# One decoder layer on one core: x loaded once, squares summed on TensorE, gates in four column groups, memory keys 512 wide, heads five chunks apart

## The chip, the cores and the metric

The kernel runs on 1 core of one Trainium2 chip. The metric is the device time of one execution in microseconds (us); the kernel before takes 1358.43 us, the median of 3 runs (1358.29 to 1359.12). A difference of 0.2% (2.7 us) is about the least that a measurement of this kernel can tell from none.

## What is computed

One inference step of a hybrid decoder layer, for 256 prompt tokens and 8 x 4 decode tokens together (288 columns), model width 2048:

```python
h = rms_norm(x, norm_mix); proj = h @ w_in          # qk_m, v_m, o_m, 4+4 gates, q_a, k_a, v_a
qk_m = silu(conv(qk_m)); h_m, C, n, m = mlstm_chunkwise(q_m, k_m, v_m, ig, fg, C0, n0, m0)   # 4 heads
h_m = rms_norm(h_m) * sigmoid(o_m)
a_out = window attention of q_a, k_a (both QK-normed), v_a, with sinks and relative bias
x = x + concat(h_m, a_out) @ w_out
x = x + cross_attend(rms_norm(x), mem_k, mem_v)     # mem_k = rms_norm(rms_norm(mem) @ wk), mem_v likewise
x = x + square(relu(rms_norm(x) @ w_up)) @ w_down   # d_ff 8192
```

Besides y it returns the new states (conv rows, C, n, m, window keys and values, memory keys and values).

## The kernel before

Activations lie transposed in SBUF (features on partitions, 16 feature tiles "kt" by 288 tokens). All weights come as a **stream** of 388 chunks of 512 KB (four 128 x 256 tiles each), in the order in which they are used. A float32 product is made of three fp32r products: each chunk is split into whi (ACT, line 1010) and wlo (DVE, line 1467, the residue), each activation tile into hi (ACT, line 992) and lo (DVE, line 1453). One chunk is then 4 kt x 3 products x 2 output tiles = 24 matmuls of 288 columns (PE, `chunk`, line 520). Four chunks make one pair of output tiles, held in PSUM banks `g`; DVE copies them out (with the factor rstd). The chunk ring has 4 places.

The order is written by hand. Each engine runs a loop over chunks c. In turn c, which I call **slot c**, PE multiplies chunk c and then does what the table `beside[c]` lists; ACT and DVE first split chunk c+3 (ACT waits until PE has released chunk c-1, and for the DMA) and then do their part of `beside[c]`; at the end of every fourth slot DVE copies out the finished tiles. Each engine takes its own instructions strictly in order, so whatever stands late in one slot holds up the split of the next.

Chunks 0 to 7 are the memory keys (`wk_x`; tokens on the output's partitions, so matmuls are 256 wide here), chunks 8 to 11 the attention keys and values (the first use of x), 12 to 27 the queries, 28 to 59 conv, q/k and values of the mLSTM heads, 60 to 75 the output gate, 76 to 107 `w_out`. Beside the first of them stand these steps:

- `mem_prep`, `x_prep(kt)`: hi and lo of a tile of the memory tokens and of x. PE waits tile by tile for them in the first chunks of each (`each`). x_prep stands two to a slot in slots 2 to 9.
- `x_squares`, slots 10 to 12: the token sums of x squared, by ACT from a second copy of x with tokens on partitions (`xtok`, `xdec`); DVE puts them on a diagonal, and `norm_x` (slot 12) spreads them over the partitions by one matmul; ACT takes the root (line 997), DVE the reciprocal (line 1456) into `rstd`.
- `gates_mm` (slot 12): 32 matmuls with hi and lo of x; then `gates_a` (DVE, ends with `nz`, line 1453), `gates_ln` (ACT: Exp, then Ln), `gates_b`, `gates_c` (DVE), `gates_exp` (ACT, ends `gate_rows`).
- `k_norm` (slot 15): ACT squares the keys, PE sums them by a matmul with `blk`, ACT root, DVE reciprocal; then `keys_turn` (17), `keys_rev` (19; both transpose keys, DVE copies them between), `columns` (20).

The mLSTM heads h stand at slots 60+4h: `m_exps`, `m_scores(h)` with `m_turn` and `m_gate` of head h-1, then `m_num(h)` one slot later, `m_state`, `m_root`, and `m_expo(h+1)` in the fourth. m_num(h) uses a PSUM bank that m_gate(h-1) reads. On DVE the split of slots 64, 68 and 72 stands after m_scores' operations and not first (`heads`). After the last output tile x is loaded again for the residual by POOL (`xT_in`); DVE waits for it when the first pair of w_out's tiles is ready.

The SP queue issues the stream, mixed with memory tokens (2 MB), x (2.25 MB), gate weights, constants, the second copy of x (2.25 MB) and the memory's second copy; a chunk's load waits for the split that frees its place.

## Time and profile before

| | us |
|---|---|
| median of 3 runs | 1358.43 |
| the profiled execution's own time | 1360.29 |
| its span on the core | 1358.5 |
| PE, DVE, ACT, POOL busy | 1330.5, 819.9, 622.7, 97.7 |
| 388 splits on DVE, on ACT, busy | 476.1, 408.5 |
| granted clock of TensorE, mean | 0.999 |

The span is one execution on the core; 1.8 us of the profiled time lie outside it. Busy times overlap between engines. Matmul ends are modelled: starts are what to read, and two matmuls of 288 columns start 0.27 us apart in a full stream. A row in brackets names what ended the idle time before an instruction.

### The profile page before, as it was taken

The numbers are of one execution on the slowest core, as the hardware profiler recorded it, in microseconds if no ns is written. First come the engines' busy times: TensorE is split into PE (matmuls) and PEld (weight loads), VectorE is DVE, ScalarE is ACT, GpSimd is POOL, SyncE is SP. The second block draws the span as 40 slices with busy tenths as digits, with TensorE's granted clock in tenths as the row PEclk, the third lists the DMA queues.
The fourth block names the chain that finished last, engine by engine and source line by source line (L and its number), as shares of the span: only waits on it lengthen the run. The fifth ranks groups of instructions, "written<-read, shape, count | busy, mean of one in ns | idle before, by whom it ended". The sixth has DMA issues, their size and how long they took to land.

```text
span 1358.5 us, 27261 instructions
## 1 busy us (share of the span) xinstructions
PE 1330.5 (98%) x10213; PEld 1301.3 (96%) x10213; DVE 819.9 (60%) x1240; ACT 622.7 (46%) x889; POOL 97.7 (7%) x139
## 2 busy tenths in 40 slices
PE   7999999999999997999999999999999999999999
PEld 7998989978999987999999999999999999999999
DVE  7767888888666466665444565444555444565443
ACT  7674666667444455543333343333343333343331
POOL 0031001111423202000000000000000000000000
PEclk9999999999999999999999999999999999999999
DMA  9687445665944963655545555555555545555543
GB/s 381 254 227 249 132 140 184 192 216 171 374 157 154 292 224 105 216 157 168 170 162 162 168 157 170 171 161 163 168 157 169 170 158 166 165 160 171 170 158 128
DMA packets 75276, 251.87 MB, mean 185 GB/s; under 512 B 8332, under 2 KB 17376, under 8 KB 74560
## 3 DMA queue, kind: packets, MB, share of 16 engines
q1 hardware_dynamic: 59184, 215.49, 48.3%
q0 software_dynamic: 15744, 35.07, 8.2%
q8 instruction: 40, 0.66, 0.2%
q10 hardware_dynamic: 288, 0.48, 0.1%
q14 instruction: 20, 0.16, 0.0%
HBM read 238.00 MB, written 13.63 MB: 185 GB/s over the span
## 4 chain that ended last, share of the span: by engine, by line
PE 80%; DVE 10%; ACT 4%; issue 3%; DMA 3%; SPq 0%; DVEq 0%; ACTq 0%
PE g L520 77%; PE m L520 3%; DVE arena L1453 3%; DMA raw<-in_stream 2%; DVE wlo L1467 2%; ACT arena L992 2%; DVE arena L1450 2%; ACT whi L1010 1%; DVE b_lo L1453 0%; DVE arena L1446 0%; DVE arena L1442 0%; DMA arena<-in_memT 0%; ACT a_hi L992 0%; DVE arena L1456 0%; ACT b_hi L992 0%
## 5 line engine op out<-in xcount | busy, mean ns | idle before, releaser
L1467 DVE TENSOR_TENSOR wlo<-raw,whi 128x1024 fp32r<-128x1024 f32 x388 | 476.1, 1237 | 375.4 <-ACT whi L1010 363.4
L1010 ACT ACTIVATE whi<-raw 128x1024 fp32r<-128x1024 f32 x388 | 408.5, 1060 | 475.3 <-PE g L520 438.6
L520 PE MATMUL g<-a_hi,whi 128*128 128x288 f32 x1632 | 355.7, 299 | 1.5 <-ACT a_hi L992 1.5
L520 PE MATMUL g<-a_lo,whi 128*128 128x288 f32 x1632 | 349.7, 295 | 0.0
L520 PE MATMUL g<-a_hi,wlo 128*128 128x288 f32 x1632 | 348.4, 295 | 0.0
L520 PE MATMUL g<-b_hi,whi 128*128 128x288 f32 x1344 | 289.3, 297 | 5.6 <-DVE arena L1450 5.4
L520 PE MATMUL g<-b_lo,whi 128*128 128x288 f32 x1344 | 288.0, 295 | 0.0
L520 PE MATMUL g<-b_hi,wlo 128*128 128x288 f32 x1344 | 286.5, 294 | 0.0
L520 PEld LDWEIGHTS g<-a_hi,whi 128*128 128x128 f32 x1632 | 261.0, 188 | 8.4 <-issue 5.4
L520 PEld LDWEIGHTS g<-a_lo,whi 128*128 128x128 f32 x1632 | 261.8, 188 | 0.0
L520 PEld LDWEIGHTS g<-a_hi,wlo 128*128 128x128 f32 x1632 | 261.8, 188 | 0.0
L520 PEld LDWEIGHTS g<-b_hi,whi 128*128 128x128 f32 x1344 | 214.9, 188 | 7.1 <-DVE wlo L1467 6.2
L520 PEld LDWEIGHTS g<-b_hi,wlo 128*128 128x128 f32 x1344 | 215.6, 187 | 0.0
L520 PEld LDWEIGHTS g<-b_lo,whi 128*128 128x128 f32 x1344 | 215.2, 188 | 0.0
L992 ACT ACTIVATE b_hi<-arena 128x288 f32 (+1 forms) x72 | 32.1, 446 | 109.3 <-DVE arena L1453 99.9
L1450 DVE TENSOR_TENSOR arena<-arena,g 128x288 f32 (+1 forms) x96 | 43.5, 453 | 48.6 <-PE g L520 42.5
L520 PE MATMUL m<-arena 128*64 128x128 f32 (+14 forms) x608 | 58.3, 335 | 5.6 <-DVE arena L1450 3.2
L520 PEld LDWEIGHTS m<-arena 128*32 128x32 f32 (+6 forms) x608 | 38.5, 141 | 19.2 <-issue 9.9
L992 ACT ACTIVATE a_hi<-arena,gcol 128x288 fp32r<-128x288 f32 (+1 forms) x48 | 25.7, 535 | 39.5 <-DVE arena L1450 37.1
L1453 DVE SCALAR_TENSOR_TENSOR arena<-g,rstd 128x288 f32<-128x288 f32 x64 | 29.3, 457 | 23.8 <-PE g L520 22.7
L1450 DVE TENSOR_TENSOR b_lo<-arena,b_hi 128x288 f32 (+1 forms) x72 | 33.0, 459 | 16.5 <-ACT b_hi L992 8.0
L992 ACT ACTIVATE arena<-arena 128x288 f32<-128x288 f32 (+9 forms) x65 | 36.7, 565 | 11.4 <-DVE arena L1450 6.9
(181 smaller groups left out, 691.9 us busy)
## 6 DMA issues: line engine op xcount, KB each, us to landing
raw<-in_stream SPq DMA_DIRECT2D x388, 512.0 KB, 3.5
arena<-in_state_C POOLq DMA_DIRECT2D x8, 512.0 KB, 5.4
out_s_C<-arena POOLq DMA_DIRECT2D x8, 512.0 KB, 3.8
arena<-in_kdT POOLq DMA_DIRECT2D x8, 512.0 KB, 17.0
arena<-in_cache_mem_v POOLq DMA_DIRECT2D x8, 512.0 KB, 8.9
arena<-in_xT SPq DMA_DIRECT2D x4, 576.0 KB, 8.4
arena<-in_xT POOLq DMA_DIRECT2D x1, 2304.0 KB, 9.7
arena<-in_memT SPq DMA_DIRECT2D x4, 512.0 KB, 7.2
```

Of the source, the lines that this page charges most:

```text
L520: return pe.matmul(out, lhsT, rhs, start=start, stop=stop, skip_group_check=True)
L992: return act.activation(out, in_, func, **kw)
L1010: act.activation(whi[:, s], raw[:, s], ACT.Copy).then_inc(sem["hi_done"], 1)
L1450: return dve.tensor_tensor(out, a, b, op)
L1453: return dve.scalar_tensor_tensor(out=out, in0=a, scalar=s, in1=b, op0=op0, op1=op1)
L1467: dve.tensor_tensor(wlo[:, s], raw[:, s], f32(whi[:, s]), SUB).then_inc(sem["chunk_split"], 1)
```

## The change

1. **SP order.** x is loaded behind the memory tokens without a wait; x's second copy is gone. The first chunk comes in halves, the memory tokens in seven pieces.
2. **Start.** PE first makes four matmuls on zeros (`warm`). ACT and DVE prepare the first chunk half by half, and mem_prep two tiles to a slot.
3. **Memory keys.** The stream's first 8 chunks hold 2 kt by 512 columns; a chunk is 12 matmuls of 512 columns. DVE copies the two tiles out in four copies at the end of slot 7.
4. **x.** x_prep stands in slots 5 to 11 (2, 2, 2, 3, 3, 3, 1). Squares of x are made from the transposed x: POOL 3 pieces, ACT 5 (128 x 576 each); `x_sums` (slot 12) sums them over partitions and kt by 16 float32 matmuls of 32 output columns in four column groups, ACT copies the sum, `norm_x` (now slot 13) adds the groups and spreads them.
5. **Gates.** `gates_mm` (slot 11) takes x itself in float32: 16 matmuls of 32 output columns in four column groups, ACT copies, `gates_sum` (slot 12) adds the groups. gates_a, _ln, _b, _c and _exp stand one slot later; gates_a has four operations fewer. k_norm stays in slot 15 but is listed after gates_ln.
6. **Heads.** They stand at slots 60+5h, `m_expo(h+1)` in the fifth; the last head runs into w_out's first chunks, where m_turn and m_gate of head 3 come after the fourth, and the first two pairs of w_out end one after the other. DVE's split stands first in every slot. POOL loads x back in two pieces.

```diff
-W_FIRST = ((0, 8), (0, 12), (1, 8), (1, 12), (0, 0), (0, 4), (1, 0), (1, 4))
+W_FIRST = ((0, 8), (0, 12), (1, 8), (1, 12), (0, 0), (1, 0), (0, 4), (1, 4))
...
+            load(raw[:, 0, 0:2].rearrange("p a b -> p (a b)"), ins["stream"][0][:, 0:half], sem["raw_ready"][0])
+            mem(0)
+            load(raw[:, 0, 2:4].rearrange("p a b -> p (a b)"), ins["stream"][0][:, half:2 * half], sem["first_raw"])
+            for b in range(1, 4):
                 chunk(b, ins["stream"][b], None)
-                load(memT[:, CK * b:CK * b + CK, :], ins["memT"][:, CK * b:CK * b + CK, :], sem["mem_in"][b])
-            for b in range(4):
...
+            for c in range(RING, 4 * RING):
+                chunk(c % RING, ins["stream"][c], c - RING + 1)
+                if c < 6:
+                    mem(c + 1)
+                if c == 6:
+                    x_load(0)
+                if c == 7:
                     load(wg_raw[:, :, :], ins["gates"], sem["wg_in"])
-            for c in range(2 * RING, 4 * RING):
...
+                if 7 <= c < 10:
+                    x_load(c - 6)
+                if c == 9:
                     load(cst[:, :], consts, sem["cst_in"])
...
+                if c >= 14:
+                    load(memtok[:, c - 14, :], ins["mem_prompt"][0, (c - 14) * P:(c - 13) * P, :], sem["mtok_in"][c - 14])
...
-        for kt in range(12, KT):
-            beside[0].append(("mem_prep", kt))
+        beside = {c: [] for c in range(4 * WOUT + 5)}
+        for kt in range(6, KT):
+            beside[kt // 2 - 3].append(("mem_prep", kt))
         for kt in range(KT):
-            beside[2 + kt // 2].append(("x_prep", kt))
+            beside[(5, 5, 6, 6, 7, 7, 8, 8, 8, 9, 9, 9, 10, 10, 10, 11)[kt]].append(("x_prep", kt))
         beside[7].append(("gate_weights",))
-        for j in range(3):
-            beside[10 + j].append(("x_squares", j))
-        for c, what in ((12, "norm_x"), (12, "gates_mm"), (13, "gates_a"), (14, "gates_ln"), (15, "gates_b"),
-                        (16, "gates_c"), (17, "keys_turn"), (17, "gates_exp"), (19, "keys_rev"), (20, "columns"),
+        for j in range(8):
+            beside[(6, 6, 7, 8, 9, 10, 11, 11)[j]].append(("x_squares", j))
...
-            at = 60 + 4 * h
+            at = 60 + 5 * h
             if h:
...
-            beside[at + 3] += [("m_root", h), ("m_state", h, 1), ("m_expo", h + 1)]
+            beside[at + 3] += [("m_root", h), ("m_state", h, 1)]
+            beside[at + 4].append(("m_expo", h + 1))
...
+            def warm():
+                pe.wait_ge(sem["dve_once"], before["warm_ready"] + 1)
+                for _ in range(4):
+                    mm(M[3][:, 0:256], rstd[:, 0:P], rstd[:, 0:256])
...
+            def mem_chunk(c):
...
+                        pe.wait_ge(sem["first_hi"] if k == 0 else sem["hi_done"], 1)
+                    pe.wait_ge(sem["mem_hi"], kt + 1)
+                    for i, (w, a) in enumerate(((whi, act_hi[1]), (whi, act_lo[1]), (wlo, act_hi[1]))):
+                        if i == 1:
...
+                            pe.wait_ge(sem["first_lo"] if k == 0 else sem["chunk_split"], 1)
+                        for j in range(2):
+                            m = mm(G[2 + j][:, :], a[:, kt, j * P:(j + 1) * P],
+                                   w[:, s, 2 * k:2 * k + 2, :].rearrange("p a b -> p (a b)"), kt == 0 and i == 0,
+                                   kt == KT - 1 and i == 2)
+                            if kt == KT - 1 and i == 2 and j == 0:
+                                m.then_inc(sem["tile0_done"], 2)
+                m.then_inc(sem["chunk_used"], 1)
...
                 s = c % RING
...
             def norm_x():
+                pe.wait_ge(sem["act_once"], before["ssum_out"] + 1)
+                mm(M[0][:, 0:NT], ones, ssum).then_inc(sem["pe_once"], 1)
...
+            def x_sums():
                 pe.wait_ge(sem["cst_in"], 16)
-                pe.wait_ge(sem["dve_once"], before["diag_ready"] + 3)
-                mm(M[0][:, 0:NT], ones, diag).then_inc(sem["pe_once"], 1)
+                pe.wait_ge(sem["x_add"], 3)
+                pe.wait_ge(sem["act_once"], before["x_sqr"] + 5)
+                for k in range(4):
+                    for i in range(4):
+                        m = mm(M[0][32 * i:32 * i + 32, 0:NT], ones[:, 0:32], xq2[2 * k + i // 2][:, i % 2, :], k == 0, k == 3)
+                m.then_inc(sem["pe_once"], 1)
...
             def gates_mm():
...
-                pe.wait_ge(sem["dve_once"], before["wg_split"] + 3)
-                for kt in range(KT):
-                    half, k = divmod(kt, 8)
-                    w = wgx[:, half, MH * k:MH * k + P]
-                    for i, a in enumerate((act_hi, act_lo)):
-                        m = mm(M[1][:, 0:NT], w, a[0][:, kt, :], kt == 0 and i == 0, kt == KT - 1 and i == 1)
+                pe.wait_ge(sem["dve_once"], before["wg_split"] + 2)
+                for k in range(4):
+                    for i in range(4):
+                        m = mm(M[1][32 * i:32 * i + 32, 0:NT], wgs[:, 4 * k + i, :], xT[:, 4 * k + i, :], k == 0, k == 3)
...
+                pe.wait_ge(sem["act_once"], before["gsum_out"] + 1)
+                mm(M[2][0:32, 0:NT], cst[:, C_SEL:C_SEL + 32], gsum)
+                mm(M[2][32:64, 0:NT], cst[:, C_SEL + MH:C_SEL + MH + 32], gsum).then_inc(sem["pe_once"], 1)
             def columns():
...
             def x_squares(j):
...
-                act.wait_ge(sem["act_once"], now("x_ssq"))
+                if j < 3:
+                    return
+                act.wait_ge(sem["x_in"][j // 2], 16)
+                act.wait_ge(sem["mem_lo"], KT)
+                A(xq2[j], xT[:, 2 * j:2 * j + 2, :], ACT.Square).then_inc(sem["act_once"], 1)
+                act.wait_ge(sem["act_once"], now("x_sqr"))
...
-                tt(res, M[1][64:64 + MH, 0:NT], rstd[64:64 + MH, :], MUL).then_inc(sem["dve_step"], 1)
...
-                tt(ig, ig, res, ADD).then_inc(sem["dve_step"], 1)
+                tt(ig, M[2][0:MH, 0:NT], rstd[0:MH, :], MUL).then_inc(sem["dve_step"], 1)
...
             for c in range(4 * WOUT):
-                heads = c > 60 and c % 4 == 0
-                if not heads:
-                    split(c + RING - 1)
+                split(c + RING - 1)
                 for what in beside[c]:
                     if what[0] in do:
...
-                        split(c + RING - 1)
-                if c % 4 == 3 and c // 4 != KVA or c == 4 * KVA + 4:
+                if c == 4 * KVA - 1:
...
-                    if skip == 0 and n == 0:
...
+                                do[what[0]](*what[1:])
+                    if skip == 0 and n == 3:
                         m_gate(MH - 1)
...
+            pool.wait_ge(sem["mem_hi"], 7)
+            pool.wait_ge(sem["mem_lo"], 7)
+            for j in range(3):
+                pool.wait_ge(sem["x_in"][j // 2], 16)
+                x = xT[:, 2 * j:2 * j + 2, :]
+                pool.tensor_tensor(xq2[j], x, x, ALU.mult).then_inc(sem["x_add"], 1)
...
-            move(xT, ins["xT"], sem["xT_in"])
+            for r in range(2):
+                for s in (2 * r, 2 * r + 1):
+                    pool.wait_ge(sem["c_out"][s], 32)
+                kt = slice(0, 7) if r == 0 else slice(7, KT)
+                move(xT[:, kt, :], ins["xT"][:, kt, :], sem["x_back"][r])
             pool.wait_ge(sem["cp_dma"], 64)
```

DVE between the split of chunk 8 (slot 5) and that of chunk 14, before; the names are the helper's line, operation, out<-in and shape; `a_lo` is x_prep, `COPY arena<-g 128x256` the memory keys:

```order
L1467 TENSOR_TENSOR wlo<-raw,whi 128x1024
L1453 SCALAR_TENSOR_TENSOR a_lo<-arena,gcol,a_hi 128x288 x2
L1467 TENSOR_TENSOR wlo<-raw,whi 128x1024
L1453 SCALAR_TENSOR_TENSOR a_lo<-arena,gcol,a_hi 128x288 x2
L1442 CAST wgx<-wg_raw 128x2x64
L1442 CAST wgx<-wg_raw 128x2x32
L1450 TENSOR_TENSOR wgx<-wg_raw,wgx 128x2x64
L1442 COPY arena<-g 128x256 x2
L1467 TENSOR_TENSOR wlo<-raw,whi 128x1024
L1453 SCALAR_TENSOR_TENSOR a_lo<-arena,gcol,a_hi 128x288 x2
```

And of the change, from the split of chunk 10 (slot 7):

```order
L1542 TENSOR_TENSOR wlo<-raw,whi 128x1024
L1528 SCALAR_TENSOR_TENSOR a_lo<-arena,gcol,a_hi 128x288 x2
L1566 MEMSET arena 128x512
L1525 TENSOR_TENSOR arena<-wg_raw,gcol 128x16x8
L1517 COPY arena<-g 128x256 x4
L1542 TENSOR_TENSOR wlo<-raw,whi 128x1024
L1528 SCALAR_TENSOR_TENSOR a_lo<-arena,gcol,a_hi 128x288 x3
L1542 TENSOR_TENSOR wlo<-raw,whi 128x1024
L1528 SCALAR_TENSOR_TENSOR a_lo<-arena,gcol,a_hi 128x288 x3
L1542 TENSOR_TENSOR wlo<-raw,whi 128x1024
L1528 SCALAR_TENSOR_TENSOR a_lo<-arena,gcol,a_hi 128x288 x3
L1542 TENSOR_TENSOR wlo<-raw,whi 128x1024
```

Twelve of the sixteen x tiles now stand behind the split of chunk 10 (two of them in its own slot); before, six did.

ACT from the norm's root to the keys' squares, before (`arena<-arena 4x288` are Exp and Ln, `128x288` the squares of k_norm; in brackets the semaphores waited for):

```order
L997 ACT_TABLE_LOAD [waits dve_once,pe_once]
L997 ACTIVATE rstd<-m,small 128x288 [waits act_once]
L1010 ACTIVATE whi<-raw 128x1024 [waits chunk_used,raw_ready0,act_once]
L1010 ACTIVATE whi<-raw 128x1024 [waits chunk_used,raw_ready1]
L992 ACT_TABLE_LOAD
L992 ACTIVATE arena<-arena 4x288 [waits dve_once]
L992 ACT_TABLE_LOAD
L992 ACTIVATE arena<-arena 4x288 [waits act_step]
L1010 ACTIVATE whi<-raw 128x1024 [waits chunk_used,raw_ready2,act_once]
L992 ACTIVATE arena<-arena 128x288 [waits tile_out]
```

and now:

```order
L1051 ACT_TABLE_LOAD [waits dve_once]
L1051 ACTIVATE rstd<-m,small 128x288 [waits pe_once]
L1064 ACTIVATE whi<-raw 128x1024 [waits chunk_used,raw_ready1,act_once]
L1064 ACTIVATE whi<-raw 128x1024 [waits chunk_used,raw_ready2]
L1046 ACT_TABLE_LOAD
L1046 ACTIVATE arena<-arena 4x288 [waits dve_once]
L1046 ACT_TABLE_LOAD
L1046 ACTIVATE arena<-arena 4x288 [waits act_step]
L1046 ACTIVATE arena<-arena 128x288 [waits tile_out,act_once]
```

The first table load no longer waits for PE, and no split stands between Ln and the keys' squares.

DVE in head 1, before, from the copy of the output gate's tiles (`arena<-g,rstd`) to head 0's m_gate (`arena<-m,arena 128x256`):

```order
L1450 TENSOR_TENSOR arena<-g,rstd 128x288 x2
L1453 SCALAR_TENSOR_TENSOR arena<-m,arena 128x384
L1453 SCALAR_TENSOR_TENSOR arena<-m,arena 32x4x4 x2
L1447 TENSOR_SCALAR arena<-m,small 128x128 x2
L1446 TENSOR_SCALAR arena<-m,small 128x128 x2
L1453 SCALAR_TENSOR_TENSOR arena<-arena 128x4x4 x2
L1467 TENSOR_TENSOR wlo<-raw,whi 128x1024
L1450 TENSOR_TENSOR arena<-m,arena 128x256
```

and now:

```order
L1542 TENSOR_TENSOR wlo<-raw,whi 128x1024
L1528 SCALAR_TENSOR_TENSOR arena<-m,arena 128x384
L1528 SCALAR_TENSOR_TENSOR arena<-m,arena 32x4x4 x2
L1522 TENSOR_SCALAR arena<-m,small 128x128 x2
L1521 TENSOR_SCALAR arena<-m,small 128x128 x2
L1528 SCALAR_TENSOR_TENSOR arena<-arena 128x4x4 x2
L1525 TENSOR_TENSOR arena<-m,arena 128x256
```

The split has moved ahead of the scores' operations.

## Rows read from the trace of the kernel before

**Rows 1.** The page's first part: busy time, share of the span, instructions.

```profile
PE 1330.5 (98%) x10213; PEld 1301.3 (96%) x10213; DVE 819.9 (60%) x1240; ACT 622.7 (46%) x889; POOL 97.7 (7%) x139
```

**Rows 2.** Busy time by stretch: us, PE, PEld, DVE, ACT, POOL (x), granted clock, DMA share, GB/s.

```profile
20.00:40.00 20.00, 20.00 (x164) 20.00 (x163) 17.93 (x29) 13.16 (x21) 0.00 (x0) 1.00 1.03 408
...
600.00:800.00 200.00, 200.00 (x1508) 200.00 (x1507) 104.98 (x127) 73.55 (x79) 0.00 (x0) 1.00 0.51 164
```

**Rows 3.** The chain that ended last, of the first 120 us: start, us, what.

```profile
21.55 8.55 DMA raw<-in_stream
```

**Rows 4.** Timeline of DVE: start, us, engine, line, operation, out<-in, count [idle before].

```profile
22.55 1.23 DVE L1467 TENSOR_TENSOR wlo<-raw,whi 128x1024 fp32r<-128x1024 f32 x1
...
23.69 1.06 DVE L1453 SCALAR_TENSOR_TENSOR a_lo<-arena,gcol,a_hi 128x288 fp32r<-128x288 f32 x2
...
24.79 0.88 DVE L1442 COPY arena<-g 128x256 f32<-128x256 f32 x2
...
31.34 1.23 DVE L1467 TENSOR_TENSOR wlo<-raw,whi 128x1024 fp32r<-128x1024 f32 x1 [0.34 <-ACT whi L1010]
...
41.99 1.06 DVE L1453 SCALAR_TENSOR_TENSOR a_lo<-arena,gcol,a_hi 128x288 fp32r<-128x288 f32 x2
...
53.14 1.95 DVE L1456 RECIPROCAL rstd<-rstd 128x288 f32<-128x288 f32 x1 [2.84 <-ACT rstd L997]
...
55.12 0.95 DVE L1450 TENSOR_TENSOR arena<-g,rstd 128x288 f32<-128x288 f32 x2
```

**Rows 5.** Timeline of PE, first 80 us.

```profile
7.83 0.77 PE L520 MATMUL g<-whi,b_hi 128*128 128x256 f32 x2 [7.83 <-ACT b_hi L992]
...
45.53 0.43 PE L520 MATMUL g<-a_hi,whi 128*128 128x288 f32 x2
...
50.45 0.72 PE L520 MATMUL m<-arena,cst 128*128 128x288 f32 x2 [1.56 <-DVE arena L1446]
...
65.09 0.75 PE L520 MATMUL m<-arena,cst 128*128 128x288 f32 x2
...
79.09 1.05 PE L520 MATMUL m<-cst,arena 128*128 128x128 f32 x8
```

**Rows 6.** Timeline of PE, four 32-column groups of query sums and a full matmul.

```profile
90.84 1.06 PE L520 MATMUL m<-arena,cst 128*32 128x256 f32 x10
```

**Rows 7.** Timeline of ACT between the norm's and the keys' sums.

```profile
51.24 1.28 ACT L997 ACT_TABLE_LOAD   x1 [1.81 <-issue]
...
64.61 0.43 ACT L992 ACTIVATE arena<-arena 128x288 f32<-128x288 f32 x1
```

**Rows 8.** Timeline of DVE, the gates' second step and the key copies.

```profile
65.88 0.44 DVE L1453 SCALAR_TENSOR_TENSOR arena<-arena 4x288 f32<-4x288 f32 x1
...
67.94 0.16 DVE L1450 TENSOR_TENSOR arena<-arena,gcol 4x8 f32<-4x8 f32 x1
...
76.25 1.65 DVE L1442 COPY arena<-m 128x256 f32<-128x256 f32 x4
```

**Rows 9.** Who waited for whom, PE alone, first 600 us: total, times, longest.

```profile
PE m L520 <- DVE arena L1450: 3.2, 3, 1.2
```

**Rows 10.** Timeline of PE, m_num of head 0 and of head 1.

```profile
255.40 3.90 PE L520 MATMUL m<-arena 128*128 128x257 f32 x34
...
275.74 1.46 PE L520 MATMUL m<-arena 128*128 128x257 f32 x6
...
278.37 2.70 PE L520 MATMUL m<-arena 128*128 128x257 f32 x28 [1.18 <-DVE arena L1450]
```

**Rows 11.** Timeline of DVE beside the scores of head 1.

```profile
272.90 0.95 DVE L1453 SCALAR_TENSOR_TENSOR arena<-m,arena 128x384 f32<-128x384 f32 x3
...
275.85 1.22 DVE L1467 TENSOR_TENSOR wlo<-raw,whi 128x1024 fp32r<-128x1024 f32 x1
```

**Rows 12.** Busy time by stretch around the clock's one fall.

```profile
132.00:135.10 3.10, 2.22 (x68) 1.34 (x66) 2.92 (x7) 0.38 (x1) 0.00 (x0) 1.00 0.55 181
...
135.10:138.50 3.40, 3.40 (x16) 3.04 (x17) 2.71 (x5) 2.53 (x5) 0.00 (x0) 0.50 0.30 95
```

More of the change, by code:

```diff
@@ L142, in weight_stream @@
     every = range(0, D, CK * P)
-    out = tiles(w["wk_x"][0], every, range(0, XW, CW))
+    out = [w["wk_x"][0][r:r + 2 * P].reshape(2, P, 2, CW).transpose(0, 2, 1, 3).reshape(CK * P, CW)
+           for r in range(0, D, 2 * P)]
     out += tiles(w["w_in"][0], every, (COL_KA,))
@@ L186, in gate_columns @@
 def gate_columns(w_in):
-    out = np.zeros((P, 2, 96), np.float32)
-    g = w_in[0][:, COL_G:COL_G + 2 * MH].reshape(2, 8, P, 2, MH)
-    out[:, :, 0:64] = g.transpose(2, 0, 3, 1, 4).reshape(P, 2, 64)
-    return out
+    return w_in[0][:, COL_G:COL_G + 2 * MH].reshape(KT, P, 2 * MH).transpose(1, 0, 2)
 ARENA = 18500
@@ L530, in chunk @@
                 s = c % RING
-                if first and t + 1 >= GB:
+                if first and t > 2 * KVA:
                     pe.wait_ge(sem["tile_out"], more_t + (t + 2 - GB))
@@ L1031, in mem_squares @@
                 act.wait_ge(sem["act_once"], now("rm_root"))
-            for c in range(RING - 1):
+            act.wait_ge(sem["raw_ready"][0], 16)
+            act.activation(whi[:, 0, 0:2], raw[:, 0, 0:2], ACT.Copy).then_inc(sem["first_hi"], 1)
+            act.wait_ge(sem["par_in"], 16)
+            mem_prep(0)
+            act.wait_ge(sem["first_raw"], 16)
+            act.activation(whi[:, 0, 2:4], raw[:, 0, 2:4], ACT.Copy).then_inc(sem["hi_done"], 1)
+            mem_prep(1)
+            for c in range(1, RING - 1):
                 split(c)
-                if c == 0:
-                    act.wait_ge(sem["par_in"], 16)
-                for kt in range(CK * c, CK * c + CK):
+                for kt in range(2 * c, 2 * c + 2):
                     mem_prep(kt)
@@ L1278, in w_out @@
                     split(4 * WOUT + 8 * skip + n + RING - 1, i * 8, i * 32)
-                    if skip == 0 and n == 0:
+                    if skip == 0:
+                        for what in beside.get(4 * WOUT + n, ()):
+                            if what[0] in do:
+                                do[what[0]](*what[1:])
+                    if skip == 0 and n == 3:
                         m_tanh(MH - 1)
@@ L1922, in _ @@
                         do[what[0]](*what[1:])
-                    if heads and what[0] == "m_scores":
-                        split(c + RING - 1)
-                if c % 4 == 3 and c // 4 != KVA or c == 4 * KVA + 4:
+                if c == 4 * KVA - 1:
+                    for j in range(2):
+                        if j == 0:
+                            dve.wait_ge(sem["tile0_done"], 2)
+                        else:
+                            dve.wait_ge(sem["chunk_used"], 8)
+                        for half in range(2):
+                            copy(kvm[:, j, half * CW:(half + 1) * CW],
+                                 G[2 + j][:, half * CW:(half + 1) * CW]).then_inc(sem["tile_out"], 1)
+                            dve.wait_ge(sem["tile_out"], now("tile_out"))
+                elif c > 4 * KVA and c % 4 == 3 and c // 4 != KVA or c == 4 * KVA + 5:
                     q = c // 4 if c % 4 == 3 else KVA
@@ L1965, in w_out @@
                     split(4 * WOUT + 8 * skip + n + RING - 1, i * 8)
-                    if skip == 0 and n == 0:
+                    if skip == 0:
+                        for what in beside.get(4 * WOUT + n, ()):
+                            if what[0] in do:
+                                do[what[0]](*what[1:])
+                    if skip == 0 and n == 3:
                         m_gate(MH - 1)
```

137 lines of the change are left out of this document (70 added, 67 removed).

## The prediction

> **What bounds the kernel now.** I read the page's first part, then busy times by stretch, then the chain, and at last the timelines of PE, DVE and ACT over the first 90 us and at the heads. PE is busy 98% of the span [rows 1], DVE 60%, ACT 46%. In the body 1508 matmuls fill 200 us without a gap, 24 to a chunk: 62.8 chunks, 3.18 us each, with DMA half used [rows 2]. So the time is PE's instruction stream plus the few places where PE stands idle or at half clock, and a saving elsewhere counts only there. Such places are: the start (first matmul at 7.83 [rows 5]), the norm (1.56 us idle ahead of 50.45 [rows 5]), the first heads (3.2 us in three waits for m_gate [rows 9]), and one fall of the clock to half, 135.1 to 138.5 [rows 12]. From 20 to 40 us it is otherwise: DMA is saturated at 408 GB/s [rows 2], a chunk of 512 KB takes 1.28 us, and the chain that ended last runs through the transfer that lands chunk 9 at 30.10 [rows 3]. PE was busy all the same, because the memory keys kept it so: there was no idle time behind the DMA.
>
> **Start (to the end of chunk 11).** The first chunk comes in halves and mem_prep two to a slot, so PE starts its real work at about 5.7 instead of 7.83 and, after `warm`, reaches full clock sooner. A 257-column matmul takes 0.115 us in a full stream (34 in 3.90 [rows 10]); twice the columns then 0.23, twelve of them 2.75 us a chunk against 24 x 0.115 = 2.76: the width alone gives nothing to 0.1 us a chunk. With 2.1 us of start and some 2.4 us of clock and width, PE reaches chunk 8 about 4.5 us earlier. That gain is lost at once. Ahead of chunk 10 in the queue stand the same bytes as before (ten chunks, 2 MB of memory tokens, 2.25 MB of x, constants; only 32 KB less of gate weights), on a path that is full. Chunk 9 landed at 30.10 [rows 3], so chunk 10 lands at 31.4 now too (bounds 30.0 and 31.4). Twelve x tiles now stand behind its split, six before. DVE from there: 1.2 to the split's start (30.10 to 31.34 [rows 3, 4]), split 1.14 and an x pair 1.10 (22.55, 23.69, 24.79 [rows 4]), zeros and gate weights 0.85 (my estimate from 0.88 for two 256-element copies), four key copies 1.76 (twice 0.88), then slots 8 to 10 of a split and three x pieces (1.14 + 1.60 = 2.74, in all 8.2), then 1.14 + 0.55: x_lo of tile 15 stands at 31.4 + 16.1 = 47.5. PE still has that tile of chunk 11 to do (0.8): it ends at 48.3, where chunk 12 began at 45.53 [rows 5]. Before, the last pair was done at 43.05 (41.99 + 1.06 [rows 4]). **Term 1: +2.8** (-1.5 to +4). PE idles about 3.5 us near tile 6 of chunk 9, from 35.6.
>
> **From there to the keys' sums.** The gates: 16 float32 matmuls in four column groups. Four groups and a full matmul of 256 columns together took 0.82 us in the queries' sums (90.84, next work at 91.66, recorded 1.06 [rows 6]), so groups run beside each other; a round of four at 288 columns is at most 0.57 and I take 0.5: 2.0 for the gates, 2.0 for x_sums, 0.55 for gates_sum. PE: 48.3 + 2.0 + 3.3 (chunk 12) + 2.0 + 0.55 + 3.35 (chunk 13) puts the norm's matmul at 59.5, against 50.45 [rows 5]. From it, k_norm's squares are reached along ACT and DVE: matmul to reciprocal 2.69 less the table load of 1.28, which no longer waits for PE (50.45, 51.24, 53.14 [rows 5, 7, 4]): 1.4; reciprocal 1.98; two tile copies 0.99 [rows 4]; split 1.14; five gate operations of 0.44 [rows 8]: 2.2; Exp 0.48, table load 1.30, Ln 0.47, squares 0.43 [rows 7]: 10.4 us, so the keys' matmul starts at 69.9, against 65.09 [rows 5]. PE has only 0.5 + 6.5 = 7.0 us of work in between (chunks 14, 15) and idles 3.4 us. Cause: the norm stands one slot later, and gates_ln is now ahead of k_norm in the same slot. Total shift here +4.8, so **term 2: +2.0** beyond term 1 (the shorter gates and sums, and the 1.56 us of idle time at the norm now filled, are in it). Bounds 0 and +4.
>
> **keys_rev.** gates_b and gates_c now both stand ahead of the key copies on DVE. gates_b is 65.88 to 68.10, 2.2 us [rows 8]; before, the copies ended at 77.90 (76.25 + 1.65 [rows 8]) and the reversed keys' matmuls began at 79.09 [rows 5], 1.2 us of slack. 2.2 less 1.2: **term 3: +1.0** (0 to 2).
>
> **Clock.** Before, 68 records of matmuls in 3.1 us, 0.9 us of it idle, were followed by 3.4 us at 0.50 (1.2 GHz) [rows 12], which costs up to 1.7 us. Two idle stretches of 3.5 and 3.4 us now stand in the first 70 us: **term 4: +1.3** (0 to 3.4; one fall of the seen size, partly inside waits). The Trainium skill, "TensorE: Matmul & The Clock Gate", section HAM oscillation, says that a wait for data puts the array back to half clock and that this is paid at each such wait; it speaks against this change, and by it both stretches would be paid, +3.4. No row here shows an idle stretch of that length on PE after the start, so the lower value stands. The fall at 135.1 may or may not come again as the work there is shifted: **term 5: -0.7** (0 to -1.7).
>
> **Table loads.** The root's activation starts 0.01 after its load's end (51.24 + 1.28 to 52.53, reciprocal at 53.14 [rows 7, 4]). The skill, "ScalarE: Activation LUTs", section What ACT_TABLE_LOAD costs, counts a drain besides, about 2.66 us a switch; by it Ln's load would add 1.4 to term 2 and the hidden one take as much out. The row shows no drain, and it decides.
>
> **Heads.** m_num takes 3.90 in head 0; in head 1 it is cut, 1.46 for six and, after 1.18 idle, 2.70 for 28 [rows 10]: DVE was late with the scores (0.95 at 272.90) and the split of 1.22 at 275.85 stood ahead of m_gate [rows 11]. Heads five apart put m_gate behind a chunk more and the split first. The three waits are 3.2 us [rows 9], with smaller ones of 0.8: **term 6: -4.0** (-3.2 to -4.3). At w_out the last head's m_gate runs 5.7 us (estimate, the same operations) beside some 7 us of PE: nothing; x's two pieces have over 1.5 us to spare by their bytes at the rate of [rows 2].
>
> At nothing: the squares on POOL (7% busy [rows 1]) and the 2.25 MB of x saved: that is 5.7 us of DMA, all behind chunk 10, where DMA no longer bounds PE.
>
> **Sum.** 2.8 + 2.0 + 1.0 + 1.3 - 0.7 - 4.0 = +2.4, +2.6 with small waits at the first head. The profiled execution took 1360.29, its span 1358.5; after, 1362.9 and 1361.1. The median of before is 1358.43, 1.9 below its profiled execution, so **1361.0**. The least difference that a measurement tells is 0.2%, 2.7 us.
>
> **Rivals.**
> - *x is prepared in time* (chance 0.18). If chunk 10 lands, or DVE gets to it, some 5 us earlier, PE keeps its lead of 4.5: chunk 11 ends at 41.0, the norm is earlier by as much and the keys' sums are at 62.7, 2.4 ahead of before. With term 3 and the heads: -2.4 + 1.0 - 4.0 = -5.4, less 0.7, plus small ones: 1353.2. For it: the first half chunk lands early and mem_prep is shorter. Against: 408 GB/s [rows 2] leaves nothing for an earlier landing.
> - *Column groups run one after the other* (0.04): eight rounds of 4 x 0.5 instead of 0.5, +12 us less a little idle time: 1372.8. Rows 6 speak against it.
> - *The stream falls behind, slower* (0.13). POOL's stores begin 1 to 4 us later against PE, beside chunks 22 to 32; where the ring has less than that in hand, about 3 us more: 1364. For it: DMA at 1.03 of its share in the start [rows 2]. Against: half share in the body. It decides if a chunk lands later than PE's need.
> - The sum itself is small between large terms; its own range is 1358 to 1364.5 (0.65).
>
> Chances: faster by over 0.2% from the first rival and the low edge of the forecast, 0.19; same, within 1355.7 to 1361.1, a little under half of the forecast's share and a few hundredths of others, 0.37; slower 0.44. Range 1354.5 to 1365.0.
>
> **What will show it.** Right: first real matmul near 5.7; chunk 10 landing near 31.4; PE idle in chunk 9 from about 35.6; chunk 11 ending near 48; 3.4 us idle ahead of the keys' matmul at 69.9, released by ACT; about 1 us idle at keys_rev; m_num 3.90 in every head, no wait for m_gate; granted clock 0.5 behind one idle stretch. Wrong: chunk 11 done by 42 (rival one); four gate matmuls of different groups starting 0.5 apart (rival two); waits for a chunk's landing between 80 and 120 us (rival three).

## Result and the profile after

| | before | the change |
|---|---|---|
| median of the runs, us | 1358.41 (6 runs, 1358.29 to 1359.14) | 1363.69 (6 runs, 1361.98 to 1365.43) |
| the profiled execution's own time, us | 1360.29 | 1362.98 |
| its span, us | 1358.5 | 1360.8 |
| DVE, ACT busy, us | 819.9, 622.7 | 817.4, 621.2 |

The change is slower by 0.36% (ratio 1.0036, 95% interval 1.0026 to 1.0047). The time is inside the range forecast and on the side that had the largest chance (slower, 0.44), 2.7 us above the number, which itself lay just within "same".

The profile page's first part of the change. PE is as full as before [rows 1]; the difference sits in a few waits.

```profile
PE 1333.0 (98%) x10161; PEld 1294.7 (95%) x10161; DVE 817.4 (60%) x1234; ACT 621.2 (46%) x891; POOL 102.8 (8%) x143
```

Timeline of PE of the change (start, us, engine, line, operation, out<-in, count, idle before): the first real matmul, the two waits for x, the gates, the norm's matmul, the keys' sum, the reversed keys, the decode tokens' scores, and m_num of heads 0 to 2.

```profile
5.25 0.70 PE L526 MATMUL g<-whi,b_hi 128*128 128x512 f32 x2
...
35.63 0.65 PE L526 MATMUL g<-a_hi,whi 128*128 128x288 f32 x2 [2.41 <-DVE a_lo L1528]
...
40.69 0.51 PE L526 MATMUL g<-a_hi,whi 128*128 128x288 f32 x2 [2.01 <-DVE a_lo L1528]
...
50.18 2.15 PE L526 MATMUL m<-arena 128*32 128x288 f32 x32
...
61.49 0.65 PE L526 MATMUL m<-arena,cst 128*128 128x288 f32 x2
...
71.76 0.75 PE L526 MATMUL m<-arena,cst 128*128 128x288 f32 x2 [3.26 <-ACT arena L1046]
...
86.56 1.13 PE L526 MATMUL m<-cst,arena 128*128 128x128 f32 x8 [0.65 <-DVE arena L1517]
...
127.60 1.14 PE L526 MATMUL m<-arena 64*32 64x128 f32 x64 [1.47 <-DVE arena L1517]
...
262.22 3.90 PE L526 MATMUL m<-arena 128*128 128x257 f32 x34
...
285.74 3.90 PE L526 MATMUL m<-arena 128*128 128x257 f32 x34
...
309.23 3.90 PE L526 MATMUL m<-arena 128*128 128x257 f32 x34
```

The decode tokens' scores in the kernel before:

```profile
119.51 1.14 PE L520 MATMUL m<-arena 64*32 64x128 f32 x64 [0.92 <-DVE arena L1442]
```

Against this row, [rows 5] and [rows 10], in the profiled executions: the end of chunk 11 is 4.65 us later (45.53, now 50.18), the keys' sum 6.7 (65.09, now 71.76), the reversed keys 7.5 (79.09, now 86.56), the decode scores 8.1 (119.51, now 127.60), m_num of head 0 6.8 (255.40, now 262.22), the end of the span 2.3. So 7.5 us are lost in the first 90 us and 0.6 more in a longer wait at the decode scores. Then 1.3 come back where the profiled execution of before had its fall of the clock [rows 12], and 4.5 from head 0 on: m_num is no longer cut. The 32 records at 50.18 are the 16 float32 gate matmuls in 2.1 us: the column groups do run side by side, as [rows 6] had it: 0.52 us a round of four.

Why the start is late: the chain that ended last (start, us, what), the timeline of ACT and that of DVE around the landing of chunk 10 and at the last x tile, all of the change.

```profile
21.38 11.22 DMA raw<-in_stream
```

```profile
32.67 1.06 ACT L1064 ACTIVATE whi<-raw 128x1024 fp32r<-128x1024 f32 x1 [3.30 <-DMA raw<-in_stream]
```

```profile
33.83 1.23 DVE L1542 TENSOR_TENSOR wlo<-raw,whi 128x1024 fp32r<-128x1024 f32 x1 [2.42 <-ACT whi L1064]
...
48.55 0.51 DVE L1528 SCALAR_TENSOR_TENSOR a_lo<-arena,gcol,a_hi 128x288 fp32r<-128x288 f32 x1
```

Chunk 10 lands at 21.38 + 11.22 = 32.60. DVE, idle for 2.4 us before it, then works 15.2 us to the end of tile 15 at 49.06, and PE follows 1.1 us later. That PE had been at chunk 8 at 29.87 instead of 32.79 (a lead of 2.9 us, where 4.5 were forecast) bought nothing: it stood idle twice.

The clock: busy time by stretch (columns as in [rows 2]), first of the change, then of the kernel before.

```profile
0.00:10.00 10.00, 7.45 (x20) 4.45 (x20) 3.48 (x8) 5.64 (x10) 0.20 (x4) 1.00 0.76 269
...
35.90:39.30 3.40, 2.78 (x12) 2.43 (x11) 3.02 (x8) 3.27 (x6) 0.00 (x0) 0.51 0.95 321
```

```profile
0.00:10.00 10.00, 2.17 (x10) 2.20 (x11) 3.68 (x8) 6.19 (x10) 0.20 (x4) 1.00 0.83 309
```

In this execution the clock fell once, to 1.2 GHz, between the two waits for x. The matmuls there took 0.48 a pair instead of 0.27, but PE had to wait 2.0 us behind them in any case, so this fall cost nothing. In other executions of the change the mean granted clock is lower: it goes from 0.999 (1361.98 and 1362.98) to 0.995 (1365.43). Of the kernel before, over the 43 runs that the experiments added, 30 have clock 1.000 (1357.5 to 1358.6, one 1359.3) and 13 have 0.998 or 0.999 (1358.8 to 1359.8). The profiled execution of before is one of those with a fall [rows 12]; its median, 1358.41, lies by its time with those that have none.

### The profile page after: what moved, and what is told of

Read it like the earlier page. It is cut to its first block, busy times and chain, and to the rows that moved or that the text cites. A ratio compares the mean times of both kernels' runs of the same rounds, so it can differ in the third digit from the quotient of the medians.

```text
span 1360.8 us, 27148 instructions
## 1 busy us (share of the span) xinstructions
PE 1333.0 (98%) x10161; PEld 1294.7 (95%) x10161; DVE 817.4 (60%) x1234; ACT 621.2 (46%) x891; POOL 102.8 (8%) x143
## 4 chain that ended last, share of the span: by engine, by line
PE 85%; DVE 7%; ACT 3%; DMA 2%; issue 2%; SPq 0%; DVEq 0%; ACTq 0%
PE g L526 80%; PE m L526 4%; DMA raw<-in_stream 2%; ACT arena L1046 2%; DVE arena L1528 1%; DVE wlo L1542 1%; ACT whi L1064 1%; DVE arena L1525 1%; DVE arena L1517 0%; ACT a_hi L1046 0%; DVE a_lo L1528 0%; DVE small L1799 0%; DVE arena L1521 0%; DVE small L1525 0%; PE m L791 0%
## 5 line engine op out<-in xcount | busy, mean ns | idle before, releaser
L526 PE MATMUL m<-arena 128*64 128x128 f32 (+13 forms) x640 | 59.0, 336 | 2.8 <-DVE arena L1517 2.3
L1046 ACT ACTIVATE arena<-arena 128x576 f32<-128x576 f32 (+8 forms) x67 | 35.7, 532 | 13.4 <-DVE arena L1528 7.8
## 6 DMA issues: line engine op xcount, KB each, us to landing
memh_scratch<-b_hi POOLq DMA_DIRECT2D x1, 2048.0 KB, 19.6
```

The lines of the kernel that those rows point to most:

```text
L526: return pe.matmul(out, lhsT, rhs, start=start, stop=stop, skip_group_check=True)
L1046: return act.activation(out, in_, func, **kw)
```

## Experiments

All times are medians, each with the kernel before on the same chip beside it (1358.10, 1358.07 and 1358.31 in the three sets). The column "above before" takes the median of before in the same set off; for the change itself it is +5.28. Runs of different sets are compared by it. The chance between executions in the clock makes a single median good to about 1 us, so each is read with a place in its trace.

| run | what | us | above before | ratio to before (95%) |
|---|---|---|---|---|
| h4 | heads four apart, split behind the scores | 1367.43 | +9.33 | 1.0065 (1.0052 to 1.0079) |
| h4_split | heads four apart, split first | 1368.23 | +9.92 | 1.0064 (1.0050 to 1.0078) |
| before_h5 | before, with part 6 alone | 1354.56 | -3.75 | 0.9974 (0.9963 to 0.9984) |
| x_early | eight x tiles ahead of chunk 10 | 1361.12 | +3.02 | 1.0021 (1.0012 to 1.0030) |
| k_first | k_norm ahead of gates_ln | 1361.05 | +2.95 | 1.0022 (1.0012 to 1.0032) |
| gc_late | key copies ahead of gates_c | 1365.87 | +7.56 | 1.0045 (1.0031 to 1.0059) |
| mem4 | memory in four pieces | 1363.90 | +5.83 | 1.0041 (1.0028 to 1.0055) |
| no_warm | no matmuls on zeros | 1363.52 | +5.21 | 1.0036 (1.0023 to 1.0050) |
| fill | idle places filled, wrongly placed | 1364.61 | +6.51 | 1.0045 (1.0031 to 1.0058) |
| fill2 | idle places filled | 1362.67 | +4.60 | 1.0035 (1.0022 to 1.0049) |
| best3 | the start, norm and keys reordered | 1353.93 | -4.14 | 0.9970 (0.9959 to 0.9981) |
| best4 | best3 and the queue reordered | 1353.69 | -4.38 | 0.9968 (0.9956 to 0.9981) |

### The heads: h4, h4_split, before_h5

```diff
-            at = 60 + 5 * h
+            at = 60 + 4 * h
...
-            beside[at + 4].append(("m_expo", h + 1))
+            beside[at + 3].append(("m_expo", h + 1))
...
-                    if skip == 0 and n == 3:
+                    if skip == 0 and n == 0:
```

and in h4 alone

```diff
-                split(c + RING - 1)
+                heads = c > 60 and c % 4 == 0
+                if not heads:
+                    split(c + RING - 1)
...
+                    if heads and what[0] == "m_scores":
+                        split(c + RING - 1)
```

h4: 

> The change with part 6 undone: heads at 60+4h, m_expo in the fourth slot, DVE's split behind the scores, and the last head's m_turn and m_gate behind w_out's first chunk. My theory: the three waits for m_gate in m_num and the small ones around them come back, 4.0 us slower: 1367.7, m_num of heads 1 to 3 cut in two again. Rival (the heads' waits had been hidden or are moved elsewhere by the spacing, into w_out's start): within 1.5 us of 1363.7.

h4_split: 

> The change with its heads four apart (m_expo in the fourth slot, last m_turn and m_gate behind w_out's first chunk), but DVE's split first in every slot. It tells the two halves of part 6 apart. My theory: the split ahead of m_gate was only part of the lateness (1.2 of about 2.7 us on DVE), so with four apart and the split ahead of the scores PE still waits at m_num, about 1.2 us in each of three heads: 3 to 4.5 us slower than the change, 1367. Rival (the order alone cures it, the spacing is for nothing): 1364.

before_h5 (part 6's lines of the diff, put into the kernel before): 

> The kernel before with part 6 alone: heads five chunks apart, DVE's split first, x's two pieces back, the order of w_out's first chunks; start, norm, gates and keys as before. My theory: part 6 is worth 4 us wherever the start stands, 1354.1, and parts 1 to 5 together cost the change about 9.5 us. Rival (part 6 gains only where the start has shifted the heads): 1357 to 1358.

h4 is 3.7 us slower than the change (4.1 by the column "above before"), and in its timeline of PE m_num of heads 1 to 3 is cut again (heads 1 and 2 shown):

```profile
283.47 1.46 PE L526 MATMUL m<-arena 128*128 128x257 f32 x6
285.88 2.71 PE L526 MATMUL m<-arena 128*128 128x257 f32 x28 [0.95 <-DVE arena L1525]
...
304.99 1.46 PE L526 MATMUL m<-arena 128*128 128x257 f32 x6
307.43 2.70 PE L526 MATMUL m<-arena 128*128 128x257 f32 x28 [0.98 <-DVE arena L1525]
```

h4_split has the same cut, the first six matmuls slower and the wait shorter:

```profile
284.48 1.82 PE L526 MATMUL m<-arena 128*128 128x257 f32 x6
286.90 2.70 PE L526 MATMUL m<-arena 128*128 128x257 f32 x28 [0.59 <-DVE arena L1525]
```

From the first to the second piece it is 2.41 us in h4 and 2.42 in h4_split: moving the split from behind the scores to ahead of them moves the delay and doesn't take it away. The spacing is what counts: five apart no m_num is cut. before_h5 gains 3.75 us on the kernel before (1358.31 to 1354.56), so part 6 is worth about the same with the old start. The change therefore stands 9.0 us above what part 6 alone gives (+5.28 against -3.75): that is what parts 1 to 5 cost. The profiled executions show 8.1 of it, up to the decode scores.

### The start: x_early, mem4, no_warm

```diff
-            beside[(5, 5, 6, 6, 7, 7, 8, 8, 8, 9, 9, 9, 10, 10, 10, 11)[kt]].append(("x_prep", kt))
+            beside[(5, 5, 6, 6, 6, 6, 6, 6, 7, 7, 7, 7, 8, 8, 9, 10)[kt]].append(("x_prep", kt))
```

x_early: 

> The change with x_prep in slots 5,5,6,6,6,6,6,6,7,7,7,7,8,8,9,10, so that eight tiles instead of four are ready before the split of chunk 10. My theory: the end of chunk 11 is set by what DVE does behind the landing of chunk 10, and DVE idles 2.4 us ahead of it (31.4 to 33.8), room for four more x tiles. DVE then reaches tile 12 at about 42.0 and PE ends chunk 11 at about 45.5 instead of 50.15; everything behind moves with it: 4.5 us faster than the change's 1363.7, 1359. Rival A (PE or the landing itself is the limit, DVE has slack): chunk 11 ends at 48 or later, at most 2 us gained, 1361.7 or more. Rival B (the start doesn't matter, it is given back at the keys' norm): under 0.5 us.

mem4 (`mem(b)` loads tiles 4b to 4b+3 behind chunk b, b = 0 to 3): 

> The change with the memory tokens in four pieces of four tiles, each behind one of the first four chunks, as before; the first chunk still in halves. My theory: small pieces in the first 10 us cost DMA about 1 us (269 GB/s against 309 in the first 10 us of the kernel before), chunk 10 lands at 31.5 instead of 32.6, and all behind it is 1.0 us earlier: 1362.7, although PE starts the memory chunks up to 1 us later. Rival (pieces don't matter, the 1.2 us come from the place of the constants): landing 32.3 to 32.9, 1363.7. Rival 2 (the late start counts): slower, 1364.7.

no_warm (`warm()` isn't called): 

> The change without the four matmuls on zeros at the start. My theory: the start's lead is hidden behind the landing of chunk 10: the memory chunks start at half clock and end about 1.5 us later (chunk 8 at 31.4 instead of 29.9), PE then idles so much less at chunk 9, and the time stays: within 0.7 us of 1363.7, rather below (a shorter idle stretch). Rival (the start counts): 1.5 us slower, 1365.2.

x_early ends chunk 11 at 47.2 instead of 50.2; the median is 2.3 to 2.6 us lower, where 4.5 was expected. First the clock, by stretch:

```profile
42.80:46.30 3.50, 3.50 (x17) 3.50 (x16) 3.43 (x5) 2.95 (x4) 0.00 (x0) 0.51 0.99 363
65.30:68.70 3.40, 0.23 (x2) 0.00 (x0) 2.65 (x7) 2.57 (x4) 0.00 (x0) 1.00 0.37 139
70.40:73.80 3.40, 3.40 (x17) 3.40 (x16) 2.31 (x2) 2.07 (x3) 0.00 (x0) 0.54 0.19 74
```

Both falls meet a busy PE (3.50 of 3.50 and 3.40 of 3.40 us). The first costs next to nothing all the same, as DVE's timeline and PE's at tile 15 show:

```profile
45.60 0.51 DVE L1528 SCALAR_TENSOR_TENSOR a_lo<-arena,gcol,a_hi 128x288 fp32r<-128x288 f32 x1
```

```profile
46.31 0.44 PE L526 MATMUL g<-a_hi,whi 128*128 128x288 f32 x2
```

DVE, without idle time since 37.8, has tile 15 ready at 46.11, and PE takes it up 0.2 us later and ends 1.1 us behind it, the same 1.1 as in the change. The theory was right that DVE's order sets the end of chunk 11, but its 45.5 was reckoned from tile 12 and left out that tiles 14 and 15 stand behind two more splits. The second fall does cost: it comes right behind the wait for the keys' squares, in which PE did 0.23 us of work in 3.40. From the keys' sum to the reversed keys it is 15.5 us (68.79 to 84.30) where the change takes 14.8, its wait of 0.65 included, so some 1.4 us of PE's time went there, half of it into that wait. Of the 3.0 us won at chunk 11 2.3 are left at the reversed keys.

mem4: chunk 10 does land earlier, ACT gets it at 31.14 instead of 32.67 (first fence). But little is seen of the theory's reason: the first 10 us move 281 GB/s (second fence), hardly more than the change's 269 and less than the 309 of before; at 30 us mem4 is 0.14 MB ahead, which at 407 GB/s is 0.3 us of the 1.5. Where the rest comes from isn't shown:

```profile
31.14 1.06 ACT L1061 ACTIVATE whi<-raw 128x1024 fp32r<-128x1024 f32 x1 [1.93 <-DMA raw<-in_stream]
```

```profile
0.00:10.00 10.00, 7.22 (x16) 5.32 (x17) 2.90 (x8) 5.04 (x8) 0.20 (x4) 1.00 0.77 281
```

```profile
30.88 1.23 DVE L1539 TENSOR_TENSOR wlo<-raw,whi 128x1024 fp32r<-128x1024 f32 x1
32.02 1.07 DVE L1525 SCALAR_TENSOR_TENSOR a_lo<-arena,gcol,a_hi 128x288 fp32r<-128x288 f32 x2
33.12 1.23 DVE L1539 TENSOR_TENSOR wlo<-raw,whi 128x1024 fp32r<-128x1024 f32 x1
```

And DVE (third fence, without idle time ahead of its split) had got the work of its earlier slots later too: its split of chunk 10 starts at 33.12 against 33.83. Of the 1.5 us 0.7 are left. In this execution they are lost as well, since the clock fell on a busy PE from 40.9 on, DVE then waited 1.2 us for ACT and PE, and chunk 11 ended at 50.55. The time, 1363.90, doesn't tell mem4 from the change. Memory in small pieces is thus not the main cause; whether 0.7 us would be won in a run without a fall stays open.

no_warm: PE reaches chunk 8 at 29.91; with the matmuls on zeros it was 29.87. They gain nothing even there, since PE, when warmed, waits 1.42 us for the second chunk's split; the total is the same too. The expected 31.4 for chunk 8 was a miss, the total not.

### The norm and the keys: k_first, gc_late

```diff
-        beside[15].append(("k_norm",))
+        beside[15].insert(0, ("k_norm",))
```

k_first: 

> The change with k_norm listed ahead of gates_ln in slot 15. My theory: the 3.3 us that PE waits for ACT's squares at 71.76 come from Exp, Ln and Ln's table load standing ahead of them. The squares then run at about 67.0, before PE arrives at 68.3; the wait is gone, and the gates' row work comes 2 us later but under cover: 3.3 us faster, 1360.4, and the wait of 0.8 at keys_rev may grow by up to 1.5. Rival A (the wait is due to the norm's late root, the tile copy being what the squares wait for): the squares stay later than 70 and under 1 us is gained. Rival B (the wait moves on): it appears at keys_rev or at the columns in full, net 0, 1363.7.

gc_late (in slot 17 `keys_turn` is listed ahead of `gates_c`): 

> The change with keys_turn ahead of gates_c in slot 17, so that DVE's key copies come before the second half of the gates. My theory (term 3): the wait of 0.9 us at keys_rev goes and nothing else changes, 1362.8. Rival (the wait moves to columns or to the first scores): 1363.7.

Timeline of PE of k_first, the norm's matmul, the keys' sum and the first transposes behind it, and ACT's squares:

```profile
62.97 0.65 PE L526 MATMUL m<-arena,cst 128*128 128x288 f32 x2
69.83 0.65 PE L526 MATMUL m<-arena,cst 128*128 128x288 f32 x2
76.69 0.82 PE L654 MATMUL m<-cst,arena 128*128 128x128 f32 x6
```

```profile
67.86 0.43 ACT L1046 ACTIVATE arena<-arena 128x288 f32<-128x288 f32 x1
```

No idle time is left: 6.86 us from the norm to the keys' sum, where the change takes 10.27 (61.49 to 71.76). Of these 3.4 us 2.3 to 2.6 arrive in the median; the wait at the reversed keys grows from 0.65 to 1.00 us. The cause, gates_ln (Exp, Ln and Ln's table load) ahead of the squares, is shown. The prediction named a second one beside it, the norm one slot later. It costs nothing here: in k_first the end of chunk 11 (51.67) and the keys' sum are 18.2 us apart, in the kernel before 19.6 (45.53 to 65.09 [rows 5]).

gc_late is slower in the median, against both theories. In its timeline of PE the wait at the reversed keys is gone, as expected, and DVE's key copies end at 87.89, 2.5 us ahead of PE:

```profile
90.44 1.05 PE L526 MATMUL m<-cst,arena 128*128 128x128 f32 x8
```

```profile
86.24 1.65 DVE L1517 COPY arena<-m 128x256 f32<-128x256 f32 x4
```

A fall of the clock behind the keys' sum (from 74.8) delayed PE there too, by 1.7 us at most, which is less than those 2.5; so it is the edit that takes the wait away. By stretch the clock was also low for 10 us in the start, at a place that the edit doesn't touch:

```profile
37.40:47.80 10.40, 8.03 (x34) 7.71 (x34) 9.28 (x16) 7.55 (x13) 0.00 (x0) 0.52 0.89 343
```

Its five runs go from 1362.02 (clock 0.997) to 1367.15 (0.995). The local gain of 0.7 us is smaller than what the clock takes by chance, and the ratio's interval overlaps that of the change. Whether the edit has a part in the lower clocks can't be told from five runs; it stays open.

### The clock: fill and fill2

```diff
+            def fill(x, n):
+                for _ in range(n):
+                    mm(M[3][:, 0:256], x[:, 0:P], x[:, 0:256])
...
+                    if c == 9 and k == 2:
+                        fill(rstd, 5)
+                    if c == 9 and k == 0:
+                        fill(rstd, 5)
...
+                fill(cst, 7)
                 pe.wait_ge(sem["k_sq"], 1)
```

(fill has `c == 10 and k == 0` with 4 in place of the second.)

fill: 

> The change with 16 float32 matmuls of 256 columns into an unused bank put where PE idles: five ahead of tile 6 of chunk 9, four ahead of tile 8 of chunk 10, seven ahead of the keys' sum (each 0.43 us at full clock, so they fit into the idle time). My theory: the spread of the change's times (1362.0 to 1365.4, clock 0.999 down to 0.995) is falls of the clock behind idle stretches; with the stretches filled, the clock stays at 0.999 or above in every run, the spread shrinks below 1 us and the median falls by 0.5 to 1.5 us, to about 1362.5. Rival A (the falls come from elsewhere, behind 118 us): clocks and spread as before, median 1363.7. Rival B (the fillers do not fit): slower by up to 2 us, 1365.7.

fill2: 

> The change with 17 dummy matmuls (float32, 256 columns, 0.43 us each) into an unused bank in the three places where it really idles: five ahead of tile 4 of chunk 9, five ahead of tile 6 of chunk 9, seven ahead of the keys' sum. (In the run fill, the first of these was left empty and four stood in front of tile 8, where PE has no idle time; they cost their 1.7 us.) My theory: every run's clock is 0.999 or 1.000 instead of 0.995 to 0.999, and the time falls by what falls of the clock cost the change in its median run: 1.0 to 2.0 us, 1362.2, with a spread under 1.5 us. Rival (falls are random and have nothing to do with idle time): clocks 0.995 to 0.999 and 1363.7 as the change.

fill missed its aim: it left the first wait (at tile 4 of chunk 9) empty and put four matmuls where PE had work. Its clocks (0.997 to 1.000) were nevertheless above the change's. fill2, timeline of PE:

```profile
33.24 2.32 PE L526 MATMUL m<-rstd 128*128 128x256 f32 x10
...
35.85 0.50 PE L526 MATMUL g<-a_hi,whi 128*128 128x288 f32 x2 [0.29 <-DVE a_lo L1537]
...
37.52 2.32 PE L526 MATMUL m<-rstd 128*128 128x256 f32 x10
...
40.91 0.50 PE L526 MATMUL g<-a_hi,whi 128*128 128x288 f32 x2 [1.08 <-DVE a_lo L1537]
```

Every run of fill2 has clock 0.999 or 1.000, its profiled one 1.000, with the waits themselves still there (chunk 11 ends at 50.39, the keys' sum starts at 71.96). So most falls of the clock here come from the idle stretches. What they cost is less sure: fill2's median is 1.0 us below the change's, 0.7 by "above before", and the intervals of the two ratios overlap almost wholly. The change's own two executions at 0.999 lie 1.2 us below its median on average. About 1 us in the median, over the stretches' own length, is an estimate from these. The Trainium skill, "TensorE: Matmul & The Clock Gate", section HAM oscillation, says that the array falls back to half clock at each such wait for data. The traces agree in part: of the seven kernels that keep the wait of 3.3 us ahead of the keys' sum unfilled (the change, x_early, h4, mem4, h4_split, no_warm, gc_late), four show the clock at half within 1.5 us behind it and three (the change, h4, h4_split) don't.

### Together: best3 and best4

best3 has the edits of x_early, k_first and gc_late, and

```diff
-        beside[7].append(("gate_weights",))
+        beside[10].append(("gate_weights",))
...
-                if c == 4 * KVA - 1:
+                if c == 4 * KVA + 2:
```

(the four key copies at the end of slot 10). best4 adds mem4's pieces and issues x's last quarter behind chunk 10 and the constants behind chunk 11.

best3: 

> The change with x_prep early (as in x_early), k_norm ahead of gates_ln, keys_turn ahead of gates_c, and the four key copies and the gate weights moved from slot 7 to slot 10. My theory: no work stands between the split of chunk 10 and tile 13 that PE doesn't need, tile 12 is ready at 39 to 40, when PE comes; PE doesn't idle in the start, chunk 11 ends at 43.5 to 44.5 (50.2 in the change), no idle ahead of the keys' sum, none at keys_rev, and with no idle stretch the clock is 0.999 or 1.000: 6.2 + 3.2 + 0.9 + 1.5 = 11.8 us faster than 1363.7, 1352, and 6 us faster than before. Rival (each gain turns up again as a wait further on, at the ring, at x_sums or at the norm's root): 1357 or more.

best4: 

> As best3, and also the memory in four pieces, and x's last quarter and the constants issued behind chunks 10 and 11. My theory: chunk 10 lands about 3.5 us earlier, but with best3 PE is bound by its own stream in the start, so this is worth at most 0.5 us over best3. Rival (best3 still waits for chunk 10): 2 to 3 us faster than best3. Rival 2 (x's last quarter comes too late for tile 12): slower than best3.

Timeline of PE of best3: the last two tiles of chunk 11, the gates, the norm's matmul, the keys' sum and the reversed keys.

```profile
41.94 0.51 PE L526 MATMUL g<-a_hi,whi 128*128 128x288 f32 x2 [0.45 <-DVE a_lo L1528]
...
44.18 0.51 PE L526 MATMUL g<-a_hi,whi 128*128 128x288 f32 x2 [1.20 <-DVE a_lo L1528]
...
45.15 2.15 PE L526 MATMUL m<-arena 128*32 128x288 f32 x32
...
56.44 0.65 PE L526 MATMUL m<-arena,cst 128*128 128x288 f32 x2
...
63.30 0.65 PE L526 MATMUL m<-arena,cst 128*128 128x288 f32 x2
...
77.19 1.05 PE L526 MATMUL m<-cst,arena 128*128 128x128 f32 x8
```

Chunk 11 ends at 45.15, 5.0 us before the change's; 1.65 us of waits for x are left (0.45 and 1.20), where none was expected. The keys' sum is at 63.30 and the reversed keys at 77.19, 9.4 before the change's. The median is 1353.93, 4.1 us below the kernel before and, by "above before", 9.4 below the change. 1352 was expected; the waits left are most of the difference. best4's 1353.69 isn't told from it, as expected; nor are both from before_h5's 1354.56. In the profiled executions, all three with clock 1.000, best3 is 2.1 us ahead of before_h5 at the reversed keys (77.19, 79.31) but 1.0 ahead at the decode scores (118.14, 119.18), where its wait is 1.45 and that of before_h5 0.37: half of what the start wins ends in a wait. With its order mended the new start costs nothing, and gains 1 us at most over the old one.

## Why the prediction was right, and where not

- **Term 1, +2.8; measured +4.65.** The mechanism stood: the lead of PE was worth nothing, DVE's work behind chunk 10's landing set the end. Two sizes were off. "Chunk 10 lands at 31.4 now too" failed, it landed at 32.60: the same bytes stand ahead of it, but the first 10 us moved 269 GB/s where before moved 309, 0.4 MB less, or 1.0 of the 1.2 us at 408 GB/s. That the smaller pieces are the reason is likely but not shown: mem4, with before's pieces of memory but the first chunk still in halves, moved 281. The rest is 0.35 us in DVE's chain and 0.3 in PE's tail. The place was wrong too: PE waited at tile 4 of chunk 9 (from 33.2) and again at tile 6, not once from 35.6. The lead at chunk 8, put at 4.5, was 2.9; being hidden, it changed nothing.
- **Term 2, +2.0; measured 6.67 - 4.65 = +2.0.** From the end of chunk 11 to the keys' sum 21.6 us were forecast and 21.58 measured, the wait 3.4 and 3.26. k_first shows that gates_ln is the cause; the other one named, the norm's later slot, costs nothing there. No extra 1.4 us behind a table load is seen: ACT reached the squares in the time of the rows.
- **Term 3, +1.0; measured 0.65 to 0.8**, gone in gc_late and, with no fall of the clock, in best3.
- **Term 4, +1.3.** In the profiled execution nothing, because the fall lay between two waits. In the median about 1, by the estimate from fill2 and the change's own executions.
- **Term 5, -0.7; measured -1.3 in the profiled execution, nothing in the median.** The fall at 135 us didn't come again; the change is 8.1 us behind ahead of it and 6.8 behind it.
- **The step from the profiled execution to the median.** The profiled time was forecast at 1362.9 and came out at 1362.98. That is luck: term 1 was too small by 1.9, terms 4 and 5 came out lower than forecast by 1.3 and 0.6, and 0.6 more of wait at the decode scores, which no term had, met 0.5 more of gain in the heads. The median was then taken 1.9 us lower because before's was, and here the forecast left the measurement: 1361.0 against 1363.69. Before's difference is its own fall of the clock, which its median doesn't have; so the change couldn't win it back, and with idle stretches in it its median has more falls than its profile, not fewer. Added up from median to median the same terms, without term 5 and with the small waits, give +3.3 or 1361.7, and the 2.0 that are then missing are the 1.9 of term 1. So the two errors that count are this step and the size of term 1; the profiled time only hid the second.
- **Term 6, -4.0; measured -3.7 to -4.1 (h4), -3.75 (before_h5) and -4.5 between the two profiled executions.** That the split's place alone would do is refuted by h4_split.
- **The rivals.** x wasn't prepared in time, the column groups ran side by side, and no wait for a chunk's landing shows between 80 and 120 us, on PE or on ACT. What was put at nothing (the squares on POOL, w_out, the bytes saved) shows no wait of PE's.

## What to carry to other kernels

A lead for the busiest engine is worth something only if the next thing that it needs comes earlier too: write down, for the first place where data arrive, which engine works behind that arrival and what stands in its order there, and move what is not needed out of that stretch. Where two steps share a slot, list first the one for which the bounding engine waits. Before a profiled time is turned into a median, look whether the profiled run holds an event, such as a fall of the clock, that the median run lacks.
